# Paged attention with interleaved gate chunks: 33 chunks stand one turn earlier, from turn 0 to turn 33

## What is computed

```python
q, k, v, u, ga, gp = jnp.split(h @ w_in, SPLITS, axis=-1)   # input projection
# samples: attention over 1024 cached positions, in 8 pages of 128 of every sample
k_past = k_cache[layer, page_table]
v_past = v_cache[layer, page_table]
s = concat(q @ k_past, q @ k_new) * scale
p = softmax(s)[..., 0] - lam * softmax(s)[..., 1]
o = p @ (v_past, v_new)
```

## Time and profile before

| | before |
|---|---|
| median of 3 runs | 2111.15 us |
| profiled execution, device time | 2112.47 us |
| profiled execution, span | 2110.6 us |
| TensorE matmul, busy | 2081.7 us (99%) |
| TensorE weight load, busy | 1908.6 us (90%) |
| VectorE, busy | 1052.7 us |
| ScalarE, busy | 676.3 us |
| GpSimd, busy | 497.5 us |
| DMA, mean over the span | 88 GB/s |

### The profile page before, as it was taken

How to read it: one execution, slowest core, us unless ns; L and a number is a source line. 1 busy time by engine, 2 the same in 40 slices (tenths; PEclk the granted TensorE clock), 3 DMA queues, 4 the chain that set the end, 5 groups by cost and what they waited for, 6 DMA issues and landing times.

```text
span 2110.6 us, 34524 instructions
## 1 busy us (share of the span) xinstructions
PE 2081.7 (99%) x13505; PEld 1908.6 (90%) x13505; DVE 1052.7 (50%) x1397; ACT 676.3 (32%) x1328; POOL 497.5 (24%) x378
## 2 busy tenths in 40 slices
PE   9999999999999999999999999999999999999999
PEld 8788888888898998999999988999899899999997
DVE  5766666666410101366552433555555455555556
ACT  5444444444443433224112412321221122122120
POOL 5432333332110101342332101311221122122120
PEclk9999999999999999999999999999999999999999
DMA  5222121212277888211224410211120111011112
GB/s 150 57 57 63 41 57 33 61 47 81 82 265 274 302 287 265 71 41 57 80 76 142 145 47 20 60 41 32 51 61 28 45 50 42 31 50 61 31 41 97
DMA packets 174560, 185.78 MB, mean 88 GB/s; under 512 B 8240, under 2 KB 147260, under 8 KB 174404
## 3 DMA queue, kind: packets, MB, share of 16 engines
q1 hardware_dynamic: 162588, 174.10, 26.5%
q10 hardware_dynamic: 11824, 9.51, 1.3%
HBM read 160.57 MB, written 23.24 MB: 87 GB/s over the span
## 4 chain that ended last, share of the span: by engine, by line
PE 88%; issue 5%; POOL 2%; DVE 2%; ACT 1%; DMA 1%; SPq 0%; ACTq 0%; POOLq 0%
PE PS L1432 34%; PE PS L2167 13%; PE PS L965 8%; PE PS L1930 4%; PE PS L284 4%; PE PS L286 4%; PE PS L285 4%; PE PS L318 3%; PE PS L342 3%; PE PS L1020 3%; PE PS L331 2%; PE PS L1035 2%; PE PS L1074 1%; PE PS L297 1%; POOL fw_lo L1419 1%
## 5 line engine op out<-in xcount | busy, mean ns | idle before, releaser
L1419 POOL TENSOR_TENSOR fw_lo<-fw_raw,fw_hi 128x1024 fp32r<-128x1024 f32 x86 | 215.6, 2506 | 885.2 <-ACT fw_hi L1415 852.2
L1432 PE MATMUL PS<-m_hi,fw_hi 128*128 128x384 f32 (+1 forms) x1032 | 228.5, 329 | 2.8 <-issue 2.8
L1432 PE MATMUL PS<-m_lo,fw_hi 128*128 128x384 f32 (+1 forms) x1032 | 227.4, 328 | 0.0
L1432 PE MATMUL PS<-m_hi,fw_lo 128*128 128x384 f32 (+1 forms) x1032 | 227.4, 328 | 0.0
L2293 DVE TENSOR_TENSOR x<-x,PS 128x512 f32<-128x512 f32 x198 | 136.1, 688 | 145.9 <-PE PS L2167 145.6
L284 PE MATMUL PS<-w_hi,act_hi 128*128 128x384 f32 (+1 forms) x520 | 188.1, 362 | 2.5 <-DVE act_lo L611 1.5
L1432 PEld LDWEIGHTS PS<-m_hi,fw_hi 128*128 128x128 f32 x1032 | 175.8, 188 | 3.9 <-issue 3.7
L286 PE MATMUL PS<-w_hi,act_lo 128*128 128x384 f32 (+1 forms) x520 | 176.5, 339 | 0.0
L1432 PEld LDWEIGHTS PS<-m_hi,fw_lo 128*128 128x128 f32 x1032 | 176.3, 188 | 0.0
L1432 PEld LDWEIGHTS PS<-m_lo,fw_hi 128*128 128x128 f32 x1032 | 176.3, 188 | 0.0
L285 PE MATMUL PS<-w_lo,act_hi 128*128 128x384 f32 (+1 forms) x520 | 176.1, 339 | 0.0
(11 more groups left out here) (303 smaller groups left out, 4199.2 us busy)
## 6 DMA issues: line engine op xcount, KB each, us to landing
k_pg<-in_cache_k_dram SPq DMA_DIRECT2D x64, 512.0 KB, 5.0
v_pg<-in_cache_v_dram SPq DMA_DIRECT2D x64, 512.0 KB, 5.1
fw_raw<-in_w_up_dram SPq DMA_DIRECT2D x44, 512.0 KB, 4.2
fw_raw<-in_w_in_dram SPq DMA_DIRECT2D x24, 512.0 KB, 5.0
wd_raw<-in_w_down_dram SPq DMA_DIRECT2D x22, 512.0 KB, 4.3
w_raw<-in_w_in_dram SPq DMA_DIRECT2D x21, 512.0 KB, 5.4
out_dram<-raw SPq DMA_DIRECT2D x16, 512.0 KB, 3.7
ga_scratch<-ga_ring ACTq DMA_DIRECT2D x8, 544.0 KB, 6.5
```

Source lines behind the costliest of these rows:

```text
L1419: e.tensor_tensor(fw_lo[slot][:, 0:kts, :], fw_raw[:, 0:kts, :], fw_hi[slot][:, 0:kts, :].bitcast(F32), ALU.subtract).then_inc(fw_tail, 1)
L1432: ins = e.matmul(PS[:, 3 * slot + c, 0:cw], w[slot][:, kt, :], x[:, kt, c0:c0 + cw], start=first and kt == 0, stop=last and kt == KT - 1)
```

## The change

The list of turns that hold a chunk becomes 0 to 30, 32 and 33, where it was 1 to 30 and 32 to 34. The chunks keep their order, so each of the 33 moves: chunk 9 from turn 1 to turn 0, and so on, chunk 38 from turn 30 to turn 29, chunk 39 from turn 32 to turn 30, chunk 40 from turn 33 to turn 32 and chunk 41 from turn 34 to turn 33. Their loads, splits and spills on SP, GpSimd and ScalarE move with them. Nothing is added to or removed from what is computed.

```diff
         V_LAG = 5
         TURNS = NB * NPG // 2 + V_LAG
-        places = [k for k in range(1, TURNS - 2) if k != NB * NPG // 2 - 1]
+        places = [k for k in range(TURNS - 3) if k != NB * NPG // 2 - 1]
         CHUNK_AT = {place: TT + i for i, place in enumerate(places)}
         assert TT + len(places) == NC * N_FILL
```

## The result

The changed kernel takes 2114.52 us (median of 15 runs, 2113.40 to 2116.67) against 2110.65 us for the kernel before (15 runs, 2108.49 to 2111.73): a ratio of 1.0021, with a 95% interval of 1.0014 to 1.0028, or 3.9 us more. That is clearly more than nothing and lies on the bound of 0.2% itself. The forecast was 2114.6 us. Among the runs of the kernel before that were made beside the experiments two took 4329.54 and 5318.55 us; these slow runs are left out of every ratio.

What follows compares the result with a forecast made beforehand. TensorE, busy for 99% of the span, was taken to bound the kernel, so only its work or idle time counts. Terms 3.38 − 1.33 + 1.4 = +3.45 us on 2111.15 gave 2114.6 us, range 2112.0 to 2117.2.

Steps and rivals of the forecast that it cites:

- Head: Start of phase 2: turn 0 gains a 384-column chunk and loses its key-bank wait, 7.22 us for 3.84, +3.38 us.
- rival D: Turn 0: its chunk waits for weights or its bank, up to 1.3 us more, 2115.9 us; chance 3%.
- turns 1 to 32: Middle of phase 2: trading chunks and moving their loads and spills costs 0 in sum.
- Tail: End of phase 2: the last values start at 842.95 instead of 844.28, −1.33 us.
- the three waits: Tail: TensorE waits 0.2, 0.9 and 2.0 us for value pages 61, 62 and 63, losing 3.1 of 4.48 us.
- the spill that leaves turn 32: Tile 12's spill moves to turn 30, relieving pages 59 and 60, which nobody was waiting for: 0.
- Rival B: Tail: page 63 lands late, from 4.7 us on making the kernel slower by over 0.2%; chance 25%.
- Clock: End of phase 2: TensorE's idling brings one stretch at half clock, +1.4 us.
- both bounds, 0 and 3.3: Tail clock cost: 0 us if it doesn't fall, 3.3 us if it falls for twice as long.
- Rival A: Tail: the clock doesn't fall despite the idle time, sum 2.05 us, 2113.2 us; chance 27%.
- Sum: Whole kernel: 3.38 − 1.33 + 1.4 = +3.45 us, giving 2114.6 us.
- Rival C: Tail: the loads are no obstacle and the bare −1.1 us comes out, 2110.0 us; chance 3%.

Runs made afterwards that it cites:

- e1: The kernel before with a chunk put into turn 0 and turn 15 left bare instead, tail chunks kept; 2109.86 us, ratio 0.9997.
- e7: The changed kernel run again, unaltered; 2114.85 us, ratio 1.0022 to the kernel before.
- e2: The kernel before with turn 34's chunk taken away and turn 31 filled, turn 0 still bare; 2114.74 us, ratio 1.0021.
- e5: The changed kernel plus unread matmuls in TensorE's idle time, 2 ahead of value page 62 and 11 ahead of page 63; 2113.46 us, ratio 1.0010.
- e8: The changed kernel with the same unread filler matmuls as e5, run again; 2111.99 us, ratio 1.0007 to the kernel before.
- e3: The changed kernel with value pages 61, 62 and 63 loaded earlier, into free key buffers; 2109.14 us, ratio 0.9995 to the kernel before.
- e9: e6 with the twelve small ffn_rows loads issued by ScalarE in turn 33 instead of by SP; 2111.65 us, ratio 1.0004 to the kernel before.
- e6: e3 with page 62 loaded in turn 31 and turn 33's chunk ahead of its value pages; 2111.35 us, ratio 1.0004 to the kernel before.

## Why the prediction was right

The time was right to 0.1 us. The head and the waits of the tail came within 0.3 us of their terms; the clock's term was 1.2 us too small.

**Head.** +3.38 forecast, +3.34 measured. No wait of the chunk in turn 0 for weights or bank (rival D), and nothing of the moved loads and spills is seen in turns 1 to 32, whose −0.23 us are more than covered by turn 31's shorter wait; e1 confirms it apart from the rest.

**Tail.** −1.33 forecast, −1.54 measured. The step "3.1 us go to the three waits" was a little too dear. The profile's two idle times add up to 2.46 us, but they count from modelled ends. From start to start, as the forecast counted, page 62 comes 0.54 us later than without a wait (forecast 1.1 with page 61's share) and page 63 another 2.30 (forecast 2.0), 2.84 in all; the other 0.1 of the tail is page 63 multiplied at the lower clock. Page 61 was not waited for; pages 61 and 62 landed after 3.8 and 4.4 us instead of 4.7 and 4.9, and page 63 after 3.6, where I took 3.9. I had put the spill that leaves turn 32 at 0, and it may be what relieved them: page 61 took 4.7 and 4.2 us in the two profiles with the spill in turn 32 and this load in its old place (before, e1), and 3.4 to 3.8 in the five with the spill moved (the change, e7, e2, e5, e8). No run tries the spill alone. The Trainium skill's fit (DMA: Bandwidth & Descriptors, section Anatomy of one DMA — SWDGE (gpsimd) path) gives 3.2 us for such a transfer, an estimate; no page came down to it: page 63 took 3.6 us here, and the shortest load of a page in all 12 profiles 3.3 (e3). Rival B's point of decision, 4.7 us for page 63, was not reached.

**Clock.** This term was mis-sized: 1.4 forecast, 2.59 measured in this profile, where the fall lasted twice as long as the one at 193 us; in e7, with one stretch of 3.41 us, new values to the first transpose of sp_rows takes 16.00 us, 1.49 more than before. I had both bounds, 0 and 3.3, and took one stretch. Its price of 1.66 us was nearly right: it set an end against a start, and from the start of L318's matmuls at 193 us to the next start of that line it is 6.37 us before (193.18 to 199.55) and 4.79 after (191.66 to 196.45), where the clock is full, so 1.58 us. Filled idle time gives back 2.6 (e5). Rival A is out: the clock fell in each profile with the waits, and no run of the change has a mean clock over 0.998. The Trainium skill (TensorE: Matmul & The Clock Gate, section Why this matters for your kernels) warns of idle gaps between bursts for this reason; in the tail the trace agrees, in each of the profiles with the waits, and two gaps in phase 1 agree only in part (last section).

**Sum.** The clock came 1.2 us dearer, the tail 0.2 and turns 1 to 32 another 0.2 cheaper, so the stage grew by 4.16 instead of 3.45. The medians give 3.87. That forecast and median agree to 0.1 us is partly luck: the growth was 0.4 us more than forecast, and the start that I added to, 2111.15 us from 3 runs, lies 0.5 above the 2110.65 of 15 runs. Besides, a stretch of half clock more or less moves the time by over 1 us from run to run.

**Rival C**, the bare −1.1 us, is what e3 shows once the loads are moved: −1.40, or −1.08 without turn 31's share. In the change itself the loads were an obstacle, and rival C is wrong.

## What to carry to other kernels

A chunk of independent work at the end of a pipelined loop may cover no engine's wait and still carry weight, as the time in which the last load lands: before taking it away, find the last use that releases a buffer, add issue and landing, and compare with what is left to run. Fetch the last pages into whatever buffer is free by then, and a bare tail costs nothing. When a small gain is taken out of a tail, look at the next thing due there (here a dozen small loads), and at what those loads hold back in their queue: with them gone from it, the next large load went out at once, beside the page that was waited for.

## What was not expected of the hardware

An idle gap of TensorE of about 2 us doesn't always bring the lower clock. Two such gaps stand in phase 1 in each of the 12 profiles. The one at 193 us, of 1.65 to 2.19 us, was followed by 3.41 us at half clock in 11 of them. The exception is the profile after, here with its clock over the same times:

```profile
191.66 0.49 PE L318 MATMUL PS<-kT,qT 64*128 64x128 f32 x4 [2.07 <-issue]
...
193.96:197.30 3.34, 3.34 (x20) 2.76 (x19) 2.12 (x7) 1.72 (x4) 1.89 (x3) 1.00 0.02 5
```

2.07 us of idling, longer than the 1.88 before, and the clock stays at 1.00. The gap at 320 us, of 1.56 to 2.10 us, was followed by 3.41 us at half clock in one profile only, that of e7, with 2.08 us. In e9 it is the longest, and the clock stays full:

```profile
321.91 0.49 PE L318 MATMUL PS<-kT,qT 64*128 64x128 f32 x4 [2.10 <-issue]
...
321.91:330.00 8.09, 8.09 (x47) 7.35 (x48) 6.17 (x12) 2.63 (x7) 4.35 (x4) 1.00 0.04 12
```

In the tail the clock fell in all five profiles with a gap of 1.64 to 2.10 us: for 3.41 us in e6 and e7, and for 6.83 in the change, e2 and e9. So the length of the gap alone doesn't decide whether the clock falls or for how long; what does stays open.
